# A hybrid decoder step on one Trainium2 core: two query convolutions placed earlier, the product with Z on GpSimd, and the output projection's two banks taken one by one

## The reference, cut to what matters

```python
def mixer(u, conv_buf, dn_buf, s0, w_in, conv_w, dn_conv_w, a_log, dt_bias, dn_norm_w, w_out):
    p = u @ w_in
    yc, new_conv_buf = causal_dwconv(gate_c * h_in, conv_buf, conv_w)
    y_conv = gate_b * yc
    qkv, new_dn_buf = causal_dwconv(p[..., OFF_QKV:OFF_Z], dn_buf, dn_conv_w)
    qkv = jax.nn.silu(qkv.astype(F32))
    q = l2norm(q) * (DN_HEAD_DIM ** -0.5)
    k = l2norm(k)
    o, s_new = gated_delta_rule(q, k, v, g, beta, s0.astype(F32))
    o = o * lax.rsqrt(jnp.mean(o * o, -1, keepdims=True) + RMS_EPS) * dn_norm_w.astype(F32)
    o = o.reshape(bsz, t, DN_WIDTH) * jax.nn.silu(z)
    mixed = jnp.concatenate([y_conv, o.astype(u.dtype)], axis=-1)
    return mixed @ w_out, new_conv_buf, new_dn_buf, s_new
```

## Time and profile before

| | |
|---|---|
| median of 3 runs | 1378.1 us (1377.1 to 1379.78) |
| the profiled execution | 1380.58 us |
| its span in the profile | 1378.7 us |
| TensorE busy | 1324.0 us, 96% |
| VectorE, ScalarE, GpSimd busy | 813.6, 550.2, 45.3 us |
| mean granted clock of TensorE | 0.98 |

### The profile page before, as it was taken

The page is one execution under the profiler, slowest core; times in us unless marked ns, Lnnn a source line. Parts: engine busy times, 40 slices in busy tenths (PEclk is TensorE's granted clock), DMA queues, the critical chain, the costliest instruction groups (busy, mean ns, idle before and its releaser), DMA issues.

```text
span 1378.7 us, 21819 instructions
## 1 busy us (share of the span) xinstructions
PE 1324.0 (96%) x9092; PEld 1097.3 (80%) x9092; DVE 813.6 (59%) x1308; ACT 550.2 (40%) x719; POOL 45.3 (3%) x102
## 2 busy tenths in 40 slices
PE   6989999989999999899998999999999999999996
PEld 2668687789999977687876999999967787876673
DVE  1667226564444447662464743644555668999896
ACT  1441113253343224321213543333344556777762
POOL 7000011000000000000200000000000000000000
PEclk9999999999999999999997999999999999999998
DMA  9644855855554552358231833734656668999991
GB/s 319 223 146 141 281 194 215 275 182 162 159 170 150 167 186 92 125 181 273 99 108 56 274 104 127 240 120 133 218 170 221 222 224 291 333 342 361 333 345 42
DMA packets 189941, 275.87 MB, mean 200 GB/s; under 512 B 7815, under 2 KB 136097, under 8 KB 184724
## 3 DMA queue, kind: packets, MB, share of 16 engines
q1 hardware_dynamic: 177856, 263.62, 57.1%
q10 hardware_dynamic: 11988, 10.86, 2.8%
HBM read 268.16 MB, written 6.30 MB: 199 GB/s over the span
## 4 chain that ended last, share of the span: by engine, by line
PE 91%; DVE 4%; DMA 2%; ACT 2%; issue 1%; SPq 0%; DVEq 0%; ACTq 0%
PE bank L1226 14%; PE bank L1012 11%; PE bank L1013 11%; PE bank L1014 11%; PE bank L1042 7%; PE bank L1044 7%; PE bank L1043 7%; PE bank L1082 4%; DMA raw<-in_w_ada_dram 2%; PE bank L1159 2%; PE bank L1598 1%; PE bank L1329 1%; PE bank L1361 1%; PE bank L1365 1%; PE bank L1470 1%
## 5 line engine op out<-in xcount | busy, mean ns | idle before, releaser
L774 DVE TENSOR_TENSOR lo_raw<-raw,hi 128x2048 fp32r<-128x2048 f32 (+2 forms) x112 | 229.4, 2056 | 99.6 <-ACT hi L1846 60.9
L1846 ACT ACTIVATE hi<-raw 128x2048 fp32r<-128x2048 f32 (+2 forms) x112 | 193.3, 1727 | 113.6 <-PE bank L1044 78.3
L1226 PE MATMUL bank<-UM,raw 128*128 128x288 f32 x864 | 223.1, 414 | 0.0
L1012 PE MATMUL bank<-UH,hi 128*128 128x288 f32 x704 | 209.8, 298 | 5.4 <-DVE UL L2259 5.1
L1014 PE MATMUL bank<-UL,hi 128*128 128x288 f32 x704 | 207.7, 295 | 0.0
L1226 PEld LDWEIGHTS bank<-UM,raw 128*128 128x128 f32 x864 | 163.1, 193 | 52.0 <-issue 8.7
L2271 DVE TENSOR_TENSOR lo<-raw,hi 128x2048 fp32r<-128x2048 f32 (+1 forms) x42 | 94.1, 2240 | 83.5 <-ACT hi L2056 48.5
L1012 PEld LDWEIGHTS bank<-UH,hi 128*128 128x128 f32 x704 | 132.6, 188 | 6.5 <-issue 4.9
L1014 PEld LDWEIGHTS bank<-UL,hi 128*128 128x128 f32 x704 | 133.2, 189 | 0.0
L1013 PE MATMUL bank<-UH,lo 128*128 128x288 f32 x432 | 128.2, 297 | 0.0
L1042 PE MATMUL bank<-hi,UGH 128*128 128x512 f32 (+9 forms) x288 | 111.7, 388 | 0.0
(11 more groups left out here) (481 smaller groups left out, 2433.9 us busy)
## 6 DMA issues: line engine op xcount, KB each, us to landing
raw<-in_w_ada_dram SPq DMA_DIRECT2D x48, 1024.0 KB, 6.8
raw<-in_w_in_dram SPq DMA_DIRECT2D x28, 1024.0 KB, 7.6
raw<-in_w_exp_gate_dram SPq DMA_DIRECT2D x26, 1024.0 KB, 5.5
raw<-in_w_exp_up_dram SPq DMA_DIRECT2D x26, 1024.0 KB, 7.6
raw<-in_w_exp_down_dram SPq DMA_DIRECT2D x16, 1024.0 KB, 5.1
raw<-in_w_exp_down_dram SPq DMA_DIRECT2D x16, 768.0 KB, 4.5
raw<-in_w_ff_gate_dram SPq DMA_DIRECT2D x11, 1024.0 KB, 5.4
raw<-in_w_ff_up_dram SPq DMA_DIRECT2D x11, 1024.0 KB, 5.4
```

The source lines that it names most:

```text
L774: dve.tensor_tensor(lo_x[g % XRAW][:, 0:XG[g][2] * XG[g][3]], x_raw(g), hi_x[g % XSPLIT][:, 0:XG[g][2] * XG[g][3]].bitcast(F32), ALU.subtr ...
L1012: pe.matmul(out, wh, xh, start=start, stop=False)
L1226: mm = pe.matmul(bank[t][:, 0:N], w_[:, d, t * P:t * P + P], UM[:, d, :], start=(d == 0), stop=(d == KT - 1))
L1846: act.activation(hi_x[q][:, 0:XG[g][2] * XG[g][3]], x_raw(g), ACT.Copy).then_inc(S("x_hi_made"), 1)
```

## The change

The list of steps gets a new kind, `cd`, the VectorE half of a convolution: that of q0 goes ahead of `sp k` and `norm k`, that of q3 ahead of `tokk`. Where a `cd` is in the list, VectorE skips the `cv`; ScalarE's half stays in its place. `cv v0` goes behind the first `X` of the solve. The product with Z is done by GpSimd, one instruction over all heads, behind `o_squared` and the eight products of line 998; `og` waits for it (`o_z`), and its second wait and the four products on VectorE are gone; ScalarE's copies wait for the bank's read instead. In the `b` tiles `w_low` comes behind the bank's products. `wo` block 0 does six k-tiles for bank 0 before it waits for bank 1, and waits for the low parts one by one.

```diff
-        s += [('sp', l, 'k'), ('norm', l, 'k')]
+        s += [('cd', l, 'q', 0), ('sp', l, 'k'), ('norm', l, 'k')]
...
         cv('q', 2)
+        s.append(('cd', l, 'q', 3))
         one('tokk')
         cv('q', 3)
...
         tile(l, 4, 1)
-        cv('v', 0)
         s += [('sp', l, 'q'), ('norm', l, 'q')]
         solve('X', 2)
+        cv('v', 0)
         tile(l, 5, 0)
...
                     op.then_inc(S("sd_decayed"), 1)
+                pool.wait_ge(S("o_squared"), l + 1)
+                pool.tensor_tensor(OT[:, :, :], OT[:, :, :], Z[:, :, :], ALU.mult).then_inc(S("o_z"), 1)
...
                         pe.wait_ge(S("lo_made"), x + 1)
-                        if s[2] == 0:
-                            fill(base, 1)
-                    fill(base, t)
+                    if (s[2], t) != (0, 1):
+                        fill(base, t)
...
-                        for ds in [W_LOW[0:3]] + [(d,) for d in W_LOW[3:]]:
-                            pe.wait_ge(S("w_split"), KT * l + W_LOW.index(ds[-1]) + 1)
+                        for ds in [W_LOW[0:6]] + [(d,) for d in W_LOW[6:]]:
                             for y in range(2):
+                                if y == 1 and ds[0] == W_LOW[0]:
+                                    fill(base, 1)
                                 for d in ds:
+                                    if y == 0:
+                                        pe.wait_ge(S("w_split"), KT * l + W_LOW.index(d) + 1)
...
                     for h in range(H):
-                        act.wait_ge(S("o_gated"), H * l + h + 1)
+                        act.wait_ge(read[(2, 3, 6, 7)[h]], base[(2, 3, 6, 7)[h]])
                         act.activation(WIH[:, CT + h, :], OT[:, h, :], ACT.Copy).then_inc(S("w_hi"), 1)
...
-                            if j > 0:
-                                w_low(l, j - 1, CH[:, j - 1, 0:N])
                             got(base, b)
                             dve.tensor_tensor(CH[:, j, 0:NP_], bank[b][:, 0:NP_], y[:, 0:NP_], ALU.mult)
...
                                               ALU.mult).then_inc(read[b], 1)
+                            if j > 0:
+                                w_low(l, j - 1, CH[:, j - 1, 0:N])
-                elif k == 'cv':
+                elif k == 'cd' or k == 'cv' and ('cd', *s[1:]) not in STEPS:
...
+                    dve.wait_ge(S("o_z"), l + 1)
                     for h, b in enumerate((2, 3, 6, 7)):
                         dve.wait_ge(full[b], base[b])
                         dve.scalar_tensor_tensor(OT[:, h, :], OT[:, h, :], nw, bank[b][:, 0:N], ALU.mult, ALU.mult).then_inc(read[b], 1)
-                    for b in (2, 3, 6, 7):
-                        dve.wait_ge(read[b], base[b])
-                    for h in range(H):
-                        dve.tensor_tensor(OT[:, h, :], OT[:, h, :], Z[:, h, :], ALU.mult).then_inc(S("o_gated"), 1)
```

## The result

The changed kernel takes 1362.5 us (median; 1362.0 to 1362.9), the kernel before, run beside it, 1378.9 us. The ratio is 0.9883, with a 95% interval of 0.9869 to 0.9897: faster by 16.4 us. The forecast was 1361.4 us. In the profiled executions the span falls from 1378.7 to 1360.7 us, by 18.0.

What follows compares the result with a forecast made beforehand. TensorE, busy 96% of the span, bounds the kernel; its stalls cost idle time plus clock lapses. Query side 9.8 and output side 8.1 make 17.9 us; 16.7 taken off the median 1378.1 gives 1361.4 us, range 1357 to 1368.

Steps and rivals of the forecast that it cites:

- the query side: TensorE's wait at the query sums and the slow tile behind: gain 4.27 us in layer 0, 5.49 in layer 1.
- the output side: TensorE's wait at the output projection's first matmul and its lapse: gain 4.2 us in layer 0, 3.85 in layer 1.
- the long lapse in layer 1: Behind the query sums: 2.79 us against 1.57 in layer 0; the extra 1.2 us need not recur in other executions.
- q3: Its convolution ahead of R lets ScalarE's copy to MT, and the query sums, come 2.70 us earlier.
- q0: Its convolution fits VectorE's idle 4.68 us ahead of `norm k`; by itself it brings TensorE nothing.
- v0: Its convolution in the old place would make `norm q` about 0.7 us late; before the first `Y`, 2.03 us is hidden.
- The sums: Query sums in each layer: of TensorE's 3.12 us wait for ScalarE's copy to MT, 0.42 us stays.
- the thin margin: VectorE's R stays in place by 0.1 us; rival: R late by up to 2 us, 1365.5 or 1368, chance 0.07.
- The first block: Output projection: 48 matmuls in 6.42 us plus about 0.15, against 8.13; bank 1 free 2.3 us before needed.
- The hold on VectorE: GpSimd's product with Z delays VectorE's convolution in layer 0 by 2.4 us; cost 0 to 0.1 us.
- The rival with GpSimd's hold: Layer 0: each us VectorE is held beyond 2.3 of slack delays TensorE one for one; 1382 us, chance 0.02.
- Loads released by TensorE's own progress: Between the changed places loads move along with TensorE, so nothing behind takes the gain back.

Runs made afterwards that it cites:

- `q3_back`: The changed kernel with q3's convolution put back behind tokk, q0 and v0 left as changed: 1372.3 us, ratio 0.9959 to the kernel before.
- `out_only`: The kernel before with only the output-side half of the change, convolutions in the old order: 1370.5 us, ratio 0.9952 to the kernel before.

## Why the prediction was right, and where it was off

**The frame held.** The change acts on two places in each layer where TensorE stood idle, each with a lapse of the clock behind it: the table of stamps gives the query side to 0.1 us and the output side of layer 1 to 0.1 us. That the total comes as close as 1361.4 to 1362.5 us is partly luck. Against 17.9 us of gain in the sum the places gave 16.7, as layer 0's output side fell short by 1.2; and the forecast took off only 16.7 for another reason, that the long lapse in layer 1 was partly chance. The traces do not settle that reason: behind an equal wait the layer 1 tile took 5.84 us in `q3_back` but 6.51 again in `out_only`. The span's 18.0 us, which look like the 17.9, hold 1.7 us of the router's clock.

**q3, q0, v0.** q3 alone brought the query side, q0 nothing, as priced. The sums keep 0.35 us, forecast 0.42. R moved by less than 0.1 us: the convolution of q3 ended at 82.80 and R began at 82.87, where it had begun at 82.42 in a trace that is 0.39 us ahead there. So the thin margin just held. For v0 the 0.7 us of each layer is measured at 0.70; that it can bring a lapse with it, 1.36 us more in layer 1, was not in the argument.

**The output block.** The first block took 6.62 us, forecast 6.57. Bank 1 was free at 225.99 and asked for at about 228.1, with 2.1 us to spare, forecast 2.3. What the sum did not see is that this spare time is the product with Z over again: either part of the change ends the stall alone, so the sum was right and its shares were not told.

**GpSimd's product, the step that failed.** The hold on VectorE was taken at 2.4 us and measured at 2.25, the product itself 2.71 us against 2.4. But its cost was put at 0 to 0.1 us, by looking at bank 1 alone. Behind the held instruction stands also ScalarE's copy of that tile, and in ScalarE's order behind that copy the norm for which `sp o` waits: 0.75 us in layer 0, shown by the copy behind the norm, where the wait goes, and by the product made twice, where it grows to 3.06. The rival with GpSimd's hold was priced one for one from 2.3 us of slack on; in fact it begins at about 1.5 us of hold, by another way, and the second 2.3 us cost 5.5, since a lapse followed.

The rule of the Trainium skill that was weighed there (SBUF — State Buffer, section Who interferes with whom) says that a VectorE instruction with two SBUF inputs contends with a GpSimd one that reads SBUF, and that the contention is an exclusive lock. The trace agrees: the product ran from 211.74 to 214.45, the last 2.46 us of it after VectorE's pair was due at 211.99, the pair was held for 2.25 us, and two products held it twice as long. Taken one engine further the rule would have given the wait at `sp o`.

**Loads released by TensorE's own progress** were taken to move with it. They nearly did; one came 0.55 us less early than TensorE, in a wait that differs by up to 0.9 us between traces with the same query side.

## What to carry to other kernels

Price a stall on TensorE by its idle time and by the slow matmuls behind it; here 10.5 us of idle time went, and the four places gained 16.7. Ask of a change with two parts aimed at one wait whether each would do alone, and follow a delayed instruction through every engine that waits for it, past what each of them has queued behind. An instruction that waits for another engine does best behind those in the same queue that wait for nothing.

## What was not expected of the hardware

The clock of TensorE fell behind a wait as short as 1.40 us in one layer, and did not behind the same wait in the other; behind equal waits of 3.1 to 3.2 us the tile that follows took 5.25, 5.36 and 5.62 us in layer 0 and 5.84, 6.51 and 6.51 in layer 1, and 7.05 behind one of 3.06 in another place. At the places of this change every one of the 13 waits of over 2 us had a lapse behind it. Its length is not settled by the wait before it, though at the output block it hardly varied: six first blocks behind waits of 2.11 to 2.65 us all took 8.11 to 8.15 us. And such a wait need not bring a lapse: behind the router's wait of 2.91 to 2.92 us the granted clock over the next 2 us was 1.00 in 4 of 14 traces and 0.50 to 0.90 in the others.
